# Hybrid SSD, attention and mixture-of-experts layer: expert weights in 2 MB transfers through a ring of ten buffers, expert bias by full-array matmuls

## The reference

```
u = rms_norm(h); proj = u @ w_in                       # projections, causal conv, SSD branch, fox attention
h = h + (gates[0]*(y_ssd @ w_ssd) + gates[1]*(y_fox @ w_fox)) @ w_out
h = h + memory_cross_attention(rms_norm(h), rms_norm(mem), w_q, w_kv, w_o)
# mixture of experts: 32 experts, each token goes to its best 4
logits = u @ w_router + b_router; top 4, softmax -> gates
for each expert e, on the tokens that chose it:
    hgl = x @ w1[e] + b1[e]                            # 1024 -> 2048
    glu = min(hgl[:, :1024], 7); lin = clip(hgl[:, 1024:], -7, 7)
    act = glu * sigmoid(1.702*glu) * (lin + 1)
    y   = act @ w2[e] + b2[e]                          # 1024 -> 1024
h = h + sum over a token's experts of gate * y
return rms_norm(h)
```

## Time and profile before

| | |
|---|---|
| time, median of 3 runs | 1413.28 us (1410.83 to 1414.98) |
| span of the profiled execution | 1406.8 us (the profile records no time outside it) |
| TensorE busy | 1349.6 us, 96% |
| DMA moved | 470.64 MB, mean 335 GB/s |
| dense part, until the first L914 | 460.07 us |
| expert part and end | 946.7 us |

### The profile page before, as it was taken

One profiled execution on the slowest core, in us unless ns is written; L12 is line 12 of the kernel. 1 busy time (PEld: TensorE's weight loads), 2 busy tenths in 40 slices (PEclk: granted clock), 3 DMA queues, 4 the chain that ended last, 5 costly groups with the idle time before them and its releaser, 6 DMA issues.

```text
span 1406.8 us, 19223 instructions
## 1 busy us (share of the span) xinstructions
PE 1349.6 (96%) x7640; PEld 730.3 (52%) x7640; DVE 421.9 (30%) x803; ACT 365.1 (26%) x557; POOL 36.7 (3%) x62
## 2 busy tenths in 40 slices
PE   6999999999999999999999999999999999999997
PEld 6999999999998333333333333333333333333332
DVE  5765666576453111211112111111111211112111
ACT  5854355644442111111111111111111111111111
POOL 3002100001001000000000000000000000000000
PEclk9999999999999999999999999999999999999999
DMA  7555544459748799999999899999999999999996
GB/s 219 151 150 150 150 120 143 152 187 335 255 147 320 312 413 418 419 418 417 417 417 419 311 409 418 419 418 418 418 416 417 418 419 418 417 416 418 418 418 266
DMA packets 136253, 470.64 MB, mean 335 GB/s; under 512 B 7496, under 2 KB 69136, under 8 KB 103408
## 3 DMA queue, kind: packets, MB, share of 16 engines
q1 hardware_dynamic: 135936, 469.73, 85.6%
q0 software_dynamic: 272, 0.27, 0.1%
HBM read 468.93 MB, written 1.05 MB: 334 GB/s over the span
## 4 chain that ended last, share of the span: by engine, by line
PE 94%; ACT 3%; issue 1%; DVE 1%; DMA 0%; SPq 0%; DVEq 0%; ACTq 0%
PE ps L914 32%; PE ps L945 16%; PE ps L580 7%; PE ps L581 7%; PE ps L582 7%; PE ps L872 4%; PE ps L887 4%; PE ps L923 4%; PE ps L879 2%; ACT arena L1213 1%; ACT arena L1201 1%; PE ps L571 1%; PE ps L572 1%; PE ps L573 1%; PE ps L936 1%
## 5 line engine op out<-in xcount | busy, mean ns | idle before, releaser
L914 PE MATMUL ps<-arena 128*64 128x512 f32 x1920 | 424.7, 594 | 0.1
L914 PEld LDWEIGHTS ps<-arena 128*64 128x64 f32 x1920 | 137.0, 137 | 279.7 <-issue 279.1
L945 PE MATMUL ps<-arena 128*64 128x512 f32 x1024 | 226.8, 595 | 24.4 <-ACT arena L1213 24.4
L1617 DVE TENSOR_SCALAR arena<-ps 128x512 f32<-128x512 f32 x32 | 22.1, 691 | 716.5 <-PE ps L914 716.5
L580 PE MATMUL ps<-A_hi,w_hi 128*128 128x256 f32 x576 | 166.7, 289 | 4.7 <-DVE A_lo L1244 3.4
L581 PE MATMUL ps<-A_lo,w_hi 128*128 128x256 f32 x576 | 163.6, 284 | 0.0
L582 PE MATMUL ps<-A_hi,w_lo 128*128 128x256 f32 x576 | 163.6, 284 | 0.0
L1277 DVE TENSOR_TENSOR w_lo<-w_raw,w_hi 128x1024 fp32r<-128x1024 f32 x120 | 143.8, 1239 | 59.2 <-ACT w_hi L1004 59.0
L945 PEld LDWEIGHTS ps<-arena 128*64 128x64 f32 x1024 | 73.1, 137 | 157.6 <-issue 157.6
L1208 ACT ACTIVATE arena<-arena 128x512 f32<-128x512 f32 x32 | 20.1, 629 | 472.7 <-DVE arena L1617 472.7
L1004 ACT ACTIVATE w_hi<-w_raw 128x1024 fp32r<-128x1024 f32 x120 | 120.3, 1048 | 26.2 <-DMA w_raw<-in_w_cross_o 7.4
(11 more groups left out here) (307 smaller groups left out, 1358.3 us busy)
## 6 DMA issues: line engine op xcount, KB each, us to landing
arena<-in_w_expert_in SPq DMA_DIRECT2D x240, 1024.0 KB, 17.7
arena<-in_w_expert_out SPq DMA_DIRECT2D x128, 1024.0 KB, 11.7
w_raw<-in_w_in SPq DMA_DIRECT2D x32, 1024.0 KB, 5.4
late<-in_w_expert_in SPq DMA_DIRECT2D x16, 1024.0 KB, 13.0
w_raw<-in_w_cross_kv SPq DMA_DIRECT2D x8, 1024.0 KB, 5.7
w_raw<-in_w_ssd_branch SPq DMA_DIRECT2D x4, 1024.0 KB, 5.0
w_raw<-in_w_fox_branch SPq DMA_DIRECT2D x4, 1024.0 KB, 5.1
w_raw<-in_w_out SPq DMA_DIRECT2D x4, 1024.0 KB, 5.6
```

The lines of the kernel that those rows point to most:

```text
L914: last = mm(ps[64 * half:64 * (half + 1), b, :], xg_cols[:, s % 4, s // 4, :], e_slot(s, outside)[:, b * DE + 512 * half:b * DE + 512 * (h ...
L945: last = mm(ps[64 * half:64 * (half + 1), 3, :], at_cols[:, k % 4, k // 4, :], e_slot(s)[:, c, 512 * half:512 * (half + 1)], start=(k == 0 ...
```

## The change

An expert is now six chunks of 2 MB: four of w1 (256 rows, two neighbouring rows in one partition, so 16 KB in one piece), and two of w2 (512 rows, four neighbouring rows of 4 KB in one partition, again 16 KB). They go through a ring of ten buffers, `W_AT`, in the order in which TensorE uses them: chunk n + 10 is issued when chunk n has been used (`refill`). The place is 20 MB as before. The first ten chunks are brought during the dense part by `piece`, in halves of 64 partitions (1 MB each): two pieces per chunk. Which rows of w1 and w2 meet in a matmul changes with it, so the transposes read every second or fourth column (`xgs[:, at + m % 2:at + 256:2]`, `lin[:, m:512:4]`) and the norm's gain is brought in that order too (`prow3`).

b1 is laid out on all 128 partitions (`b1raw`), ScalarE rounds it and VectorE puts the remainder on partitions 32 to 63 and 96 to 127 (`b1p`); per item two fp32r matmuls with all 128 columns (L885) write it, one per bank, ahead of the first product. They stand among the transposes of the item before. The order of the transposes is activations first, gathered tokens second.

Small loads change their queue: the norm and convolution parameters (8 transfers, now 9) go from SP to ACT, ahead of all other work there; eight others (w_in's narrow columns, biases, the router) go from POOL to SP, before `load(2)`. `late` is page 24 of the arena now, and `gfin` has a place of its own, so that the final norm's gain is loaded before the expert loop instead of behind it.

```diff
-            if s < 8:
-                return w_ein[0, expert, s * P:(s + 1) * P, :]
-            t = s - 8
-            return w_eout[0, expert, 2 * t * P:2 * (t + 1) * P, :].rearrange("(c p) n -> p c n", p=P)
+            if s < 4:
+                return w_ein[0, expert, 256 * s:256 * (s + 1), :].rearrange("(p c) n -> p (c n)", c=2)
+            return w_eout[0, expert, 512 * (s - 4):512 * (s - 3), :].rearrange("(p c) n -> p (c n)", c=4)
...
+            def piece(n, h):
+
+                rows = slice(64 * h, 64 * (h + 1))
+                sp_.dma_start(e_slot(n)[rows, :], e_chunk(n // CHUNKS, n % CHUNKS)[rows, :]).then_inc(e_loaded[n], 16)
...
-            ahead = [(0, 0), (0, 1), (0, 2), (0, 3), (0, 4), (0, 5), (1, 0)]
+            ahead = [(0, 0), (0, 1), (1, 0), (1, 1), (2, 0), (2, 1), (6, 0), (6, 1)]
             for u in range(unit("out", 3), unit("cv", 1)):
                 load(u)
                 if ahead:
-                    chunk(*ahead.pop(0))
+                    if ahead[0] == (6, 0):
+                        sp_.wait_ge(a_lo_ready, SPLIT["u2"] + 4)
+                    piece(*ahead.pop(0))
...
+            def refill(n, r):
+
+                at = r + SLOTS_W
+                sp_.wait_ge(e_used, n + 2)
+                sp_.dma_start(e_slot(r % SLOTS_W), e_chunk(n_expert(n, r) + at // CHUNKS, at % CHUNKS)).then_inc(e_loaded[r % SLOTS_W], 16)
...
+            def bias(b):
+
+                mm(ps[:, b, :], selb[:, :], b1p[:, b, :], start=True, stop=False, skip_group_check=True)
...
+                for s in range(4):
+                    pe.wait_ge(e_loaded[slots[s]], loads[s])
+                    w = e_slot(slots[s])
+                    for c in range(2):
                         for b in range(2):
                             for half in range(2):
-                                mm(ps[64 * half:64 * (half + 1), b, :], selb[0:NE, :],
-                                   b1[0:NE, b * DE + 512 * half:b * DE + 512 * (half + 1)], start=False, stop=False)
+                                at = 2048 * c + b * DE + 512 * half
+                                last = mm(ps[64 * half:64 * (half + 1), b, :], xg_cols[:, 2 * (s % 2) + c, s // 2, :],
+                                          w[:, at:at + 512], start=False, stop=(s == 3 and c == 1), skip_group_check=True)
+                    last.then_inc(h_psum if s == 3 else e_used, 2 if s == 0 else 1)
...
-                gathered_transposes(i + 2)
                 pe.wait_ge(act_ready, i + 1)
                 for m in range(4):
-                    last = nc.tensor.transpose(ps[:, 0, m * P:(m + 1) * P], lin[:, m * P:(m + 1) * P], idn)
+                    last = nc.tensor.transpose(ps[:, 0, m * P:(m + 1) * P], lin[:, m:512:4], idn)
                 last.then_inc(at_psum, 1)
+                gathered_transposes(i + 2)
+                pe.wait_ge(selb_ready, i + 2)
+                bias(1)
                 pe.wait_ge(at_ready, i + 1)
+                bias(0)
```

More of the change, by code:

```diff
@@ L32 @@
 NI = 64
-EARLY = 5
+CHUNKS = 6
+SLOTS_W = 10
+ROUND = 5
 EPS = 1e-6
@@ L180, in layer_program @@
         dsk, bdf = late[:, 1488:1496], late[:, 1496:1520]
[L183 to L186, removed]
+        W_AT = (0, 2, 4, 6, 8, 10, 23, 18, 14, 16)
+        prow3 = late[0:4, 1536:1792]
+        b1raw = sb("b1raw", [P, 2, 512])
+        b1p = sb("b1p", [P, 2, 512], f32r)
+        gfin = b1raw[:, :, :].rearrange("p a b -> p (a b)")
+        halves = sb("halves", [P, P])
+        selb = sb("selb", [P, P], f32r)
+        pe1x = sb("pe1x", [P, NI])
         ident = sb("ident", [P, P])
@@ L290, in layer_program @@
         ld_b1, ld_b2 = sem("ld_b1"), sem("ld_b2")
+        b1_rounded, b1_ready = sem("b1_rounded"), sem("b1_ready")
         ld_g = sem("ld_g")
[L292 to L293 removed]
+        e_loaded = [sem(f"e_loaded{s}") for s in range(SLOTS_W)]
         e_used = sem("e_used")
@@ L370, in _ @@
             load(unit("co", 2))
-            chunk(0, 6)
+            piece(3, 0)
             load(unit("co", 3))
[L373 to L378, removed]
+            piece(3, 1)
+            for h in range(2):
+                piece(7, h)
+            sp_.wait_ge(w_lo_ready, 2 * NU)
+            for h in range(2):
+                piece(8, h)
@@ L379, in _ @@
             sp_.wait_ge(w_done, 2 * NU)
[L380 to L383, removed]
+            for n in (5, 9):
+                for h in range(2):
+                    piece(n, h)
             sp_.wait_ge(item_psum, 2)
             sp_.dma_start(b2[0:NE, :], b_eout[0]).then_inc(ld_b2, 16)
[L388 to L405, removed]
@@ L419, in _ @@
+            PER = CHUNKS * ROUND
+            TURNS = (CHUNKS * NE - SLOTS_W) // PER
+            with sp_.Fori(0, TURNS) as turn_:
+                for r in range(PER):
+                    refill(PER * turn_ + r, r)
+            for r in range(CHUNKS * NE - SLOTS_W - PER * TURNS):
+                refill(PER * TURNS + r, r)
             sp_.wait_ge(meta_ready, 1)
@@ L465, in _ @@
             pool.wait_ge(consts, 12)
+            link(nc.gpsimd.memset(halves[:, :], 0.0))
+            for h in range(2):
+                rows = slice(64 * h, 64 * (h + 1))
+                link(nc.gpsimd.memset(halves[rows, rows], 1.0))
             nc.gpsimd.tensor_scalar(islot[:, :, :], iota[:, :, :], -NO_SLOT, None, ALU.add).then_inc(pool_chain, 1)
@@ L960, in _ @@
                    start=False, stop=False, skip_group_check=True)
-            with pe.Fori(NE // 4, NE // 2) as pair:
-                two_items(pair)
+            with pe.Fori(EARLY, FULL) as n:
+                turn(n, ROUND)
+            turn(FULL, NE - ROUND * FULL)
             with pe.If(n_items > NE):
                 with pe.Fori(NE, n_items) as i:
-                    item(i, False, 16 * i - 16 * (NE // 2 - 1))
+                    item(i, range(2, 2 + CHUNKS), [16 * i - 16 * (NE - 21)] * CHUNKS)
             pe.wait_ge(y_ready, n_items + 1)
@@ L1139, in _ @@
             step("ck", 0)
+            act.wait_ge(ld_b1, 64)
+            A(b1p[:, :, :], b1raw[:, :, :], ACT.Copy).then_inc(b1_rounded, 1)
             def pair_square(name, n):
@@ L1476, in _ @@
             step("ck", 0)
+            dve.wait_ge(b1_rounded, 1)
+            for at in (32, 96):
+                rows = slice(at, at + 32)
+                V_.tensor_tensor(b1p[rows, :, :], b1raw[rows, :, :], b1p[rows, :, :].bitcast(f32), ALU.subtract).then_inc(b1_ready, 1)
             for n in range(4):
```

159 lines of the change are left out of this document (74 added, 85 removed).

## The result

The changed kernel takes 1415.9 us, median of 14 runs (1411.9 to 1420.8); the kernel before took 1413.3 in as many runs beside them (1407.8 to 1415.2). The ratio is 1.0029, 95% interval 1.0017 to 1.0041: slower by 0.3%, a small difference, but its interval lies clear of 1. Forecast were 1399 us and faster, 1376 to 1413. The time is outside of the range and on the other side.

A forecast was written before the change was run, and what follows sets the result against it. DMA was taken as the bound, 30.1 us per item against TensorE's 29.3. Items at 472 + 18 backlog + 889.1 stream, then the end, gave a 1392.4 span; plus 6.5, 1399 us (1.0% faster), range 1376 to 1413.

The forecast's parts named there:

- The dense part: Before the expert items: 64-partition pieces delay cv 0, 12 of 14 us taken; items begin at 472, bounds 0 and 16.
- The piece: Early 1 MB transfer to 64 partitions: 5.43 us at 193 GB/s, bounds from 2.5 us.
- the pair: A load and a piece among the early chunks: 3.2 plus 5.43 us; nine loads and eight pieces 72 us.
- Backlog: At the first item: two loads and ten pieces still queued, so the ring's stream begins at +18 us.
- Rate: Expert weight stream: 16 KB packets at 429.3 GB/s, 182 transfers in 889.1 us; bounds 409.2 to 437 GB/s.
- both rivals on 16 KB packets: Expert stream: no better than 8 KB, 1415 us, chance 0.12; or loses rate, 1443 us, chance 0.08.
- The end: After the last transfer: 0.5 us to land, 3.55 for the last chunk's matmuls, then 9.2 unchanged to the span's end.
- Outside the span: Timed median against profiled span: 6.5 us on top, as before, making 1399 us from 1392.4.
- TensorE's item: Expert part: 26.7 us instead of 29.33, bounds 26.2 to 28.0; worth nothing beyond the lead left, 4 us.
- the lead: 20 MB of expert weights in SBUF when items begin, used up just when the work is; 4 us left.
- halves cost nothing: Rival on early pieces: 64 partitions go at full rate, items start at 460, 1377 us timed; chance 0.16.
- A dense part yet later: Within the remaining outcomes: dense part delayed beyond the forecast, or clock lost in TensorE's new waits; together 0.07.

The follow-up runs named there:

- e1_columns: The changed kernel with each of the 20 early pieces as half of a chunk's columns on all 128 partitions, not half of the partitions: 1381.97 us, ratio 0.9795.
- e8_first8_wide: The changed kernel with only the first eight early pieces as column halves on 128 partitions, the other twelve still 64-partition halves: 1387.65 us, ratio 0.9818.
- e5_packets_8_4: e1_columns with rows 128 apart in each 2 MB transfer, so 8 KB packets for w1 and 4 KB for w2; only time is read: 1403.81 us.
- e3_no_b1: The kernel before without the four matmuls that add bias b1 in each item, so its result lacks b1: 1400.3 us, ratio 0.993.

## Why the prediction was wrong

The forecast span was 1392.4 us; the profiled one is 1414.5. The 22.1 us between them, step by step:

- **The dense part: +19.6.** Items were to begin at 472 and began at 491.6. This is the step that failed. The piece itself was right: 5.43 us from the 193 GB/s of the earlier trace rows, and 203 GB/s measured alone make 5.2. Wrong was the pair, where the load beside the piece was left at the 3.2 us of before, 8.63 together: alone, with nothing that waits, a pair takes 9.5, and in the kernel eight pairs took 78.8 us, 9.8 each (from the rounding of out 3 at 323.69 to that of cv 0 at 402.47). The forecast had nine loads and eight pieces in 72 us from 314 on; it was 88. Of the 16 us between, 10 are the pairs, 2 the clock, and 4 the first load, out 3, which lands later than 3.2 us from 314 on; 3 of these 4 are in e1_columns too. The second error was in going on from there: the working itself gave 14 us, I took 12 "since waits in TensorE push loads back too", and this pushes the end back, not forward. Measured against e1_columns, the halves put the start back by 28.4, and by 29.3 with the clock set equal (ahead of all pieces, a rounding stands at 302.68 in e1_columns, at 301.78 in the changed kernel and at 299.63 before). That is outside of the bounds of 0 and 16; the upper bound had only the one price, with no room for a dearer pair. The other 2.2 us are clock, which was in no term: 29.3 - 12 + 2.2 = 19.5. (A sum beside it was off too: with 218 GB/s the wait comes to 9 us, not 8.)
- **Backlog: -6.** The ring's stream begins 12 us behind the first item (491.6 to 503.5), not 18. The ten pieces go at 211 to 221 GB/s from 460 us on, 4.9 us each and not 5.43, which is 5 us of it. It is not the late start of the items: in e8_first8_wide they begin at 462.4 and the stream 13 us behind.
- **Rate: +4.6.** 429.3 GB/s were forecast from the cost of one packet, 428 came. From 503.5 to the last landing near 1397.2 are 893.7 us instead of 889.1; at 428 GB/s the bytes alone need 892, and the rest is the thin end of the last transfers. The step was right, and both rivals on 16 KB packets fall. The 20 or so us that it was to bring are there, as e5_packets_8_4 shows.
- **The end: +4.** The last transfer of w2 was taken for what ends last, 4.05 us ahead of the end of the second product. It is the last w1 chunk: from 1388.79 it takes 3.65 us of L909, then scatter, gather, transposes and bias up to 1398.20, and 7.09 of L936, 16.5 together. w2's last chunk lands 8 us behind that chunk and waits. The order of the last six transfers was in the diff; I followed the bytes and not the path behind each.
- **Outside the span: 1.8 us, not 6.5.** I set the profiled span of before, 1406.8, against the median of three other executions. The changed kernel's span of 1414.5 belongs to a time of 1416.29, and in every execution the two are 1.7 to 1.9 apart. The other 4.7 us were the distance of a fast execution, with a clock of 1.00, from the median. So the 6.5 stood, without my knowing it, for what the clock takes in most executions, and the forecast of 1399 is 17 us off where the span is 22 off.
- **TensorE's item: right,** 26.6 for 26.7, though the two bias matmuls in it took 0.85 us and not 0.48; and worth next to nothing, as stated: the waits took its place. An item shorter by 1.86 us was worth 8 us in the kernel before (e3_no_b1), where the forecast says "a few us at most" and puts the lead at 4. The kernel lives by the transfers.

Together 19.6 - 6 + 4.6 + 4 = 22.2, the 22.1 within rounding.

The rival "halves cost nothing" had 0.16 and 1377 us. Its mechanism is false. e1_columns, the kernel in which they really do cost nothing, came at 1382, and that it is so near is luck: the rival's span was 1370.4 and the profiled one is 1381.1, 10.7 longer (3 at the first item by the clock, the rest at the end and in the stream), and the 6.5 put on top hid more than half of it. No rival held a dearer pair. "A dense part yet later" stood beside lost clock under 0.07, without a price; it is what happened.

## What to carry to other kernels

Cut a transfer across its columns and keep all 128 partitions; a cut across partitions halved the rate of the DMA engines at a full share (203 GB/s for 427), and made what shares the queue land later. When a rate is taken from a row, apply it to everything that is in the queue in that stretch, the foreign loads too, and then look whether TensorE's queue waits for one of them: of twenty halves, the eight that stood between awaited loads cost 28 to 30 us, and the other twelve 3 to 6. Take span and time from the same execution, and look at the clock of the stretches before a step of 2 or 3 us is put down to an edit.

## What the runs showed of the hardware

- 32 partitions (206 GB/s), 64 (203) and 64 upper and lower by turns (214) are nearly the same to the DMA engines, 128 give 427. That the two halves by turns do not add up was open before the run. The Trainium skill, *SBUF — State Buffer*, section "Door 1: The DMA port swizzle (why `[64,N]` ≈ `[32,N]`)", states that 64 partitions from 0 on get the bandwidth of 32, and the trace agrees.
- A load of 1 KB packets and a half by turns take 9.5 us, 1.3 more than the two prices alone; a load and a transfer to 128 partitions take 5.5, as their prices add up to.
- Packets of 8 and 4 KB, 8 and 16 KB, and 16 KB alone give 418, 424 and 428 GB/s over hundreds of us in the same kernel.
- TensorE's granted clock fell to a mean of 0.70 over 10 us (to 1.2 GHz for a part of them) with the engine 100% busy before and in that stretch, at the same place in the program, by a different amount in each execution (from 0.70 to 0.84, or not at all). By the roundings it cost 0, 1.5 or 3.0 to 3.1 us. Executions of the kernel before differ by up to 8 us with their mean clock; where the rest of that lies was not looked for.
